# Layer 0's mixer: keys and memory queries projected first, norms spread between k steps, attention in paired halves with the sample as one of its items

## What is computed

```python
z = h @ p['w_in_a'][a]
q, k, v, xq = jnp.split(z, [A_Q, A_Q + A_KV, A_Q + 2 * A_KV], axis=-1)
q = rms_norm(q.reshape(n, t, A_HEADS, HEAD_DIM), p['q_norm_a'][a])
k = rms_norm(k.reshape(n, t, A_KV_HEADS, HEAD_DIM), p['k_norm_a'][a])
v = v.reshape(n, t, A_KV_HEADS, HEAD_DIM)
if is_prompt:
    o = swa_prompt(q, k, v, slopes, p['sinks_a'][a])
else:
    o, nk, nv = swa_sample(q, k, v, win_k_in[a], win_v_in[a], slopes, p['sinks_a'][a])
...
xq = rms_norm(xq.reshape(n, t, X_HEADS, HEAD_DIM), p['xq_norm'][i])
xo = memory_attention(xq, mk, mv)
x = x + jnp.concatenate([o, xo], axis=-1) @ w_out
```

## Time and profile before

| | us |
|---|---|
| median of 3 runs | 2440.69 (2440.61 to 2445.96) |
| span of the profiled execution | 2437.8 |
| PE busy in it | 2364.8 (97%) |
| DVE, ACT, POOL busy | 1152.4, 674.6, 596.1 |

### The profile page before, as it was taken

One profiled execution on the slowest core, in us unless ns is written; L12 is line 12 of the kernel. 1 busy time (PEld: TensorE's weight loads), 2 busy tenths in 40 slices (PEclk: granted clock), 3 DMA queues, 4 the chain that ended last, 5 costly groups with the idle time before them and its releaser, 6 DMA issues.

```text
span 2437.8 us, 37784 instructions
## 1 busy us (share of the span) xinstructions
PE 2364.8 (97%) x14538; PEld 2238.3 (92%) x14538; DVE 1152.4 (47%) x2144; ACT 674.6 (28%) x1247; POOL 596.1 (24%) x413
## 2 busy tenths in 40 slices
PE   5999999999999999999999998899999999999999
PEld 5898755899999999999999997699999999999999
DVE  7213377245454455554455133415555445445554
ACT  6211277242211112222225222514222221112221
POOL 3111033342212122222224121333222221212221
PEclk9998799999999999999999998899999999999999
DMA  5213000111111111111111112011111111111112
GB/s 202 86 44 139 5 1 1 29 44 61 44 43 35 42 47 48 52 52 52 43 35 51 44 44 95 4 43 35 52 53 52 52 43 43 35 42 44 50 52 84
DMA packets 36288, 123.29 MB, mean 51 GB/s; under 512 B 5264, under 2 KB 9968, under 8 KB 34896
## 3 DMA queue, kind: packets, MB, share of 16 engines
q1 hardware_dynamic: 26208, 95.43, 12.7%
q10 hardware_dynamic: 10000, 26.76, 2.9%
HBM read 115.57 MB, written 8.63 MB: 51 GB/s over the span
## 4 chain that ended last, share of the span: by engine, by line
PE 87%; DVE 5%; issue 4%; ACT 2%; POOL 1%; ACTq 0%; DMA 0%; DVEq 0%; POOLq 0%
PE ps L449 26%; PE ps L450 26%; PE ps L451 25%; PE ps L645 2%; DVE h_lo L1258 2%; PE ps L672 2%; PE ps L578 1%; PE ps L659 1%; PE ps L610 1%; ACT s_exp L1014 1%; DVE z L1645 1%; PE ps L722 1%; PE ps L560 1%; ACT p_t L850 0%; DVE s_exp L1424 0%
## 5 line engine op out<-in xcount | busy, mean ns | idle before, releaser
L449 PE MATMUL ps<-h_hi,w_hi 128*128 128x352 f32 x3120 | 1012.7, 325 | 14.9 <-DVE h_lo L1258 5.6
L450 PE MATMUL ps<-h_lo,w_hi 128*128 128x352 f32 x3120 | 1001.5, 321 | 0.0
L451 PE MATMUL ps<-h_hi,w_lo 128*128 128x352 f32 x3120 | 1000.7, 321 | 0.0
L356 POOL TENSOR_TENSOR w_lo<-raw,w_hi 128x1024 fp32r<-128x1024 f32 x138 | 345.1, 2502 | 1497.3 <-ACT w_hi L850 1497.3
L449 PEld LDWEIGHTS ps<-h_hi,w_hi 128*128 128x128 f32 x3120 | 586.3, 188 | 36.5 <-issue 22.3
L450 PEld LDWEIGHTS ps<-h_lo,w_hi 128*128 128x128 f32 x3120 | 587.2, 188 | 0.0
L451 PEld LDWEIGHTS ps<-h_hi,w_lo 128*128 128x128 f32 x3120 | 585.9, 188 | 0.0
L1565 DVE TENSOR_TENSOR x<-x,ps 128x352 f32<-128x352 f32 x528 | 270.7, 519 | 173.9 <-PE ps L451 173.1
L449 PE MATMUL ps<-g_hi,d_hi 128*128 128x352 f32 x1056 | 340.4, 322 | 3.5 <-DVE g_lo L1558 3.5
L450 PE MATMUL ps<-g_lo,d_hi 128*128 128x352 f32 x1056 | 339.9, 322 | 0.0
L451 PE MATMUL ps<-g_hi,d_lo 128*128 128x352 f32 x1056 | 339.7, 322 | 0.0
(11 more groups left out here) (175 smaller groups left out, 1897.0 us busy)
## 6 DMA issues: line engine op xcount, KB each, us to landing
raw<-in_w SPq DMA_DIRECT2D x182, 512.0 KB, 3.6
x<-in_x_t ACTq DMA_DIRECT2D x4, 1056.0 KB, 10.0
out_y<-x ACTq DMA_DIRECT2D x8, 528.0 KB
s_mk<-in_s_mk ACTq DMA_DIRECT2D x2, 2048.0 KB, 9.5
s_mv<-in_s_mv ACTq DMA_DIRECT2D x2, 2048.0 KB, 14.6
mem_x<-in_mem_t ACTq DMA_DIRECT2D x1, 1024.0 KB, 7.0
s_k<-in_s_k ACTq DMA_DIRECT2D x2, 512.0 KB, 4.4
s_v<-in_s_v ACTq DMA_DIRECT2D x1, 1024.0 KB, 17.1
```

The lines of the kernel that those rows point to most:

```text
L356: pool.tensor_tensor(lo, raw[:, slot], hi.bitcast(F32), ALU.subtract).then_inc(prepped, 1)
L449: pe.matmul(out, a, hi_x(k), start=(first and n == 0), stop=False)
L450: pe.matmul(out, a, lo_x(k), start=False, stop=False)
L451: ins = pe.matmul(out, b, hi_x(k), start=False, stop=(last and n == len(ks) - 1))
```

## The change

The in-projection's units come in another order: keys (6, 7), memory queries (8, 9), queries (0 to 5), values (10, 11). All units from the third on write banks 0 to 2, and spreads (`spread_a`) go to banks 3 to 5 between k steps, four tiles in units 5 and 6, six in unit 11; the root is taken twice. Square sums are added inside units. Value transposes (`values_in`) come behind the first item's scores. SyncE issues the cache loads and then the window stores.

The attention has 25 items: per block two sliding-window items of 6 heads (two key heads, one in each half of the partitions) and one memory item of 4 heads, and as item 5 the sample (its four kinds of heads with queries in `q4`, 32 columns each, four samples side by side in the columns). Each item has two halves n = 2k and 2k + 1, which top, exps, scale, normalise, turn and take handle one by one. Scores of an item fill banks 0 to 3. The sink is a column of the scores, so that its maximum, exponential and sum come with the others and the small instructions for it go. Outputs go back into `z` (`evict`), and are cut into high and low parts later in pieces of 128 x 704, eight of them on ScalarE and GpSimd between items, four at the end on ScalarE and VectorE. The first two output chunks of the first output unit run between the last items, and the first six chunks come in the order (0,0), (0,1), (1,0), (1,1), (0,2), (1,2). `p_t` has three places, two of them and `k_tok` over the values in `z`, so that ScalarE waits for the store of those values (`vp_stored`) before it writes `k_tok` or `p_t`. Layer 1 keeps its work; its functions are only separated.

```diff
+NORMED_A = [[6, 7, 8, 9], [0, 1, 2, 3, 4, 5]]
+SPREAD_AT = {(5, 1, 1): 6, (5, 1, 6): 7, (5, 2, 3): 8, (6, 0, 3): 9,
+             (11, 0, 2): 0, (11, 0, 6): 1, (11, 1, 2): 2, (11, 1, 6): 3, (11, 2, 2): 4, (11, 2, 6): 5}
+STAT_AT = {(2, 1): 0, (2, 2): 1, (3, 1): 2, (4, 1): 3, (5, 1): 4, (6, 1): 5, (7, 1): 6, (8, 1): 7, (9, 1): 8,
...
+SMP_AT = 5
...
+def attn_items():
+    out = []
+    for b in range(NB):
+        out += [("swa", b, 0), ("swa", b, 1), ("mem", b, 0)]
+    out.insert(SMP_AT, ("smp", 0, 0))
+    return out
...
-        cursor[0] = r_at + 10 * size([P, T])
-        p_t = put("p_t", [P, 2, 2 * 3 * P])
...
+            for u in range(IN_A):
+                n = S_INA + u
+                sp.wait_ge(prepped, n - 1)
+                sp.dma_start(raw[:, n % 2], d["w"][S_INA + UNITS_A[u]]).then_inc(raw_landed[n % 2], 16)
+            load_units(S_OUTA // 2, S_OUTA // 2 + 1)
+            m = mx[0]
+            sp.wait_ge(proj, 3 * (R_INA + IN_A))
+            for i in range(2):
+                sp.dma_start(s_k[:, i, :, 0:BLOCK], d["s_k"][:, i]).then_inc(m["caches"], 16)
+            sp.dma_start(s_v[:, :, :], d["s_v"]).then_inc(m["caches"], 16)
+            sp.dma_start(s_mk[:, :, :, :], d["s_mk"][0]).then_inc(m["caches"], 16)
+            sp.dma_start(s_mv[:, :, :, :], d["s_mv"][0]).then_inc(m["caches"], 16)
+            sp.wait_ge(freed[(R_INA + IN_A - 1) % 2], 3 * ((R_INA + IN_A - 1) // 2) + 3)
+            sp.dma_start(o["win_v_p"], z[:, 10:12, T - BLOCK:T]).then_inc(vp_stored, 16)
+            sp.wait_ge(m["z_normed"], 30)
...
+            def spread_a(t):
+                m = mx[0]
+                idx = UNITS_A.index(t)
+                grp = 0 if t in NORMED_A[0] else 1
+                pe.wait_ge(m["z_rstd"], grp + 1)
+                if idx >= 1:
+                    pe.wait_ge(m["z_normed"], NCH * idx)
+                for c in range(NCH):
+                    pe.matmul(ps[:, 3 + c, 0:CH], sel_t[32 * c:32 * c + 32, t, :], rstd[32 * c:32 * c + 32, :],
+                              start=True, stop=True).then_inc(m["z_spread"], 1)
...
+                pe.wait_ge(prepped, n + 1)
+                for c in range(NCH):
+                    t0 = c * CH
+                    pe.wait_ge(freed[1 - s], 3 * ((r - 1) // 2) + c + 1)
+                    def between(k):
+                        if (u, c, k) in SPREAD_AT:
+                            spread_a(SPREAD_AT[u, c, k])
+                    products(ps[:, c, 0:CH],
+                             lambda k: w_hi[:, s, k * P:(k + 1) * P], lambda k: w_lo[:, s, k * P:(k + 1) * P],
+                             lambda k: h_hi[:, k, t0:t0 + CH], lambda k: h_lo[:, k, t0:t0 + CH],
+                             range(KD), landed=between).then_inc(proj, 1)
+                    if (u, c) in STAT_AT:
+                        idx = STAT_AT[u, c]
+                        first = idx in (0, len(NORMED_A[0]))
...
+            def values_in():
+                m = mx[0]
+                for q in range(6):
+                    if q >= 2:
+                        pe.wait_ge(m["turned_taken"], q - 1)
+                    bank = 6 + q % 2
+                    for b in ([2 * q, 2 * q + 1] if q < 4 else [8]):
+                        w, t0 = (BLOCK, TS + b * BLOCK) if b < 8 else (TS, 0)
+                        for t in range(2):
+                            at = ((b % 2) * 2 + t) * P
+                            mm = pe.transpose(ps[0:w, bank, at:at + P], z[:, (10 if q < 5 else 6) + t, t0:t0 + w],
+                                              ident[:, :])
...
+            def attention():
+                m = mx[0]
+                def scores(k):
+                    kind, b, i = A[k]
+                    if k >= 1:
+                        pe.wait_ge(m["ready"], 2 * k)
+                        if A[k - 1][0] != "swa":
+                            pe.wait_ge(m["exped"], 2 * k)
...
+                    if kind == "swa":
+                        w = BLOCK if b == 0 else 256
+                        k0 = q0 + BLOCK - w
+                        for j in range(3):
+                            for h in range(2):
+                                rows = slice(64 * h, 64 * h + 64)
+                                mm = pe.matmul(ps[:, 2 * h + j // 2, (j % 2) * 256:(j % 2) * 256 + w],
+                                               z[rows, 3 * i + j, q0:q0 + BLOCK], z[rows, 6 + i, k0:k0 + w],
+                                               start=True, stop=True)
+                                if j == 2:
+                                    mm.then_inc(m["scored"], 1)
...
                 def turn(n):
-                    kind, b, g = items[n]
-                    nh = 3 if kind == "swa" else 2
+                    kind, b, i = A[n // 2]
+                    h = n % 2
                     pe.wait_ge(m["normed"], n + 1)
                     if n >= 1:
                         pe.wait_ge(m["pturned_taken"], n)
                     out = banks(4, 2, 768)
...
+                def values(k):
+                    kind, b, i = A[k]
+                    pe.wait_ge(m["pturned_taken"], 2 * k + 2)
+                    if k == 0:
+                        pe.wait_ge(m["turned_taken"], 6)
+                    if k >= 2:
+                        pe.wait_ge(m["o_done"], k - 1)
...
+                    if kind == "swa":
+                        kcs = [0] if b == 0 else [0, 1]
+                        for kc in kcs:
+                            for h in range(2):
+                                g = 2 * i + h
+                                mm = pe.matmul(ps[64 * h:64 * h + 64, bank, 0:3 * P],
+                                               v_tok[:, b - len(kcs) + 1 + kc, g * HD:(g + 1) * HD],
...
+                                                   pt_sm[:, kc, cs], start=(kc == 0), stop=(kc == 1),
+                                                   skip_group_check=True)
+                    mm.then_inc(m["pv"], 1)
+                pe.wait_ge(freed[0], 3 * ((R_INA + IN_A) // 2))
+                pe.wait_ge(freed[1], 3 * ((R_INA + IN_A) // 2))
+                pe.wait_ge(m["z_normed"], NCH * len(stat_tiles(0)))
+                for k in range(M + 3):
+                    if 2 <= k < M + 2:
+                        turn(2 * k - 4)
+                    if k >= 3:
+                        values(k - 3)
+                    if k < M:
+                        scores(k)
+                    if 2 <= k < M + 2:
+                        turn(2 * k - 3)
+                    if k == 0:
+                        values_in()
+                    if k == M:
+                        pe.wait_ge(m["exped"], 2 * M)
+                        pe.wait_ge(m["o_cut"], 4)
+                        pe.wait_ge(m["o_low_pool"], 4)
+                        pe.wait_ge(prepped, S_OUTA + 1)
+                        out_a_unit(R_OUTA, 0)
+                    if k == M + 1:
+                        pe.wait_ge(m["o_cut"], 8)
+                        pe.wait_ge(m["o_low_pool"], 8)
+                        out_a_unit(R_OUTA, 1)
...
+            def attention():
+                m = mx[0]
+                def exps(n):
+                    kind, b, i = A[n // 2]
+                    h, st = n % 2, stat[:, n % 8]
+                    act.wait_ge(m["ready"], n + 1)
                     if kind == "swa":
...
+                def take(n):
+                    kind, b, i = A[n // 2]
+                    act.wait_ge(m["pturned"], n + 1)
+                    if n == 0:
+                        act.wait_ge(vp_stored, 16)
+                    out = banks(4, 2, 768)
+                    if kind == "smp" and n % 2 == 0:
+                        scopy(pt_sw[:, :, :], out[:, 0:384].rearrange("p (j n) -> p j n", j=3))
+                        ins = scopy(pt_new[:, :, :], out[0:TS, 384:768].rearrange("p (j n) -> p j n", j=3))
+                    elif kind == "smp":
+                        ins = scopy(pt_sm[:, :, :], out[:, 0:256].rearrange("p (k n) -> p k n", k=2))
+                    else:
+                        w = 512 if kind == "mem" else 384 if b == 0 else 768
+                        if n >= 3:
+                            act.wait_ge(m["pv"], (n - 3) // 2 + 1)
+                        ins = scopy(p_t[n % 3][:, 0:w], out[:, 0:w])
+                    ins.then_inc(m["pturned_taken"], 1)
...
+                act.wait_ge(m["sinks_set"], 1)
+                for k in range(M + 2):
+                    for h in range(2):
+                        if k >= 2:
+                            take(2 * k - 4 + h)
+                        if k < M:
+                            exps(2 * k + h)
+                    if k == 0:
+                        values_in()
+                    if k in SPLIT_AT:
+                        high(SPLIT_AT[k])
+                for e in range(8, 12):
+                    high(e)
...
+                def top(n):
+                    kind, b, i = A[n // 2]
+                    h, st = n % 2, stat[:, n % 8]
```

(44 more changed lines are left out.)

990 lines of the change are left out of this document (532 added, 458 removed).

## The result

The changed kernel takes 2477.4 us (median of 4 runs, 2476.0 to 2478.9) where the kernel before took 2440.7 in the same session: 1.0146 times as long, 95% interval 1.0132 to 1.0159. Slower was forecast, by 13 us; it is 36.7. The profiled execution spans 2475.1 us (before: 2437.8), so that the difference to be placed in the traces is 37.3.

What follows compares the result with a forecast made beforehand. TensorE was taken to bound the kernel before. Items to 438.9 plus 16.8 for clock falls put the output projection's first product at 455.7 against 441.5, +14.2; taken as +13 on the median 2440.7: 2454 us, range 2425 to 2475.

Steps and rivals of the forecast that it cites:

- s(k): Attention: time when item k's scores are usable; s(3) 257.5, s(9) 323.1, s(24) 429.1 us without the twelve clock falls.
- Projection: Input projection: in-line norms 8.8, square sum 0.7 and bank wait 1.7 put the last product 11.2 us later, at 227.5.
- The triples: Last projection unit: ten spreads of three matmuls between k steps, each delaying the next product 0.88 us, 8.8 in all.
- The queue of the stores: Attention start: ScalarE waits for the out_win_v_p store behind the cache loads, until 248.5 instead of 236.
- rival 2: Attention start: the store is not held up by the loads, 12 us less, 2442; chance 0.08.
- The items around the sample: Attention from s(3) 257.5 to s(9) 323.1, with 19.9 us of sample values and sample scores at a quarter of 15.8.
- The chain in a paired item: Attention: scores, top, exponentials, copy, turn, values form one loop without overlap; block 21.2 us against 18.9, idle time 3.7.
- rival 1: Attention: the clock holds, since TensorE is active 12.4 of 21.2 us; 16.8 less, 2436; chance 0.18.
- The clock: Attention: each 3.7 us idle time costs a fall, 3.4 us at half clock, losing 1.4; twelve sliding items, 16.8.
- After the last scores: End of attention: TensorE work behind s(24) apart from two output chunks, 6.1, 2.7 and 1.0, in all 9.8 us.
- (4): Attention: the clock stays at half through most of it, 29 us more, 2483; chance 0.11.
- (3): Attention: the loop is not the bound, VectorE's 15.8 us per block counts and no falls; about 2400; chance 0.11.

Runs made afterwards that it cites:

- the kernel with the three edits: Changed kernel with both p_t copies ahead of the exponentials on ScalarE, the out_win_v_p store ahead of the cache loads, and 96 unused bytes: 2414.4 us.
- the pad: Changed kernel with 96 unused bytes per partition put back where the arrays of negated sinks stood: 2465.8 us.
- the run with the two early ones: Changed kernel with unneeded matmuls in twelve sliding items' idle times and the two ahead of the sample, 96 bytes and the store ahead of the loads: 2435.8 us.

## Why the prediction was right in direction and too low in size

The loop in a paired item and the wait for the store came as forecast. What failed were sizes and one missing term. The price of the falls of the clock was too low: none was put on the idle times ahead of the sample (6.5 us low from s(3) to s(9)), and for each one behind it the stretch at half clock was taken as 3.4 us where it is 4.8 on average (5 us low in five blocks). And everything outside the mixer was put at nothing, where the moved tiles cost most of 9.1 us. In the order of the prediction's steps, with s(k) read at the end of the scores' groups:

**Projection: 11.2 forecast, 13.5 measured.** The triples cost what was said: ten intervals of 1.05 between products where 0.16 stood. Unit 2's wait for the fourth eviction is there, 1.70 of idle time at 89. What was missed is the pace: from unit 7 on, where neither memory products nor spreads stand between, a unit takes 12.49 us where it took 12.37. The place of the tiles enters here too: the kernel before takes 12.49 with its 32 bytes added, and the changed kernel 12.40 on average at +128. But it isn't all of it, nor does the place within 128 bytes decide here: with the 96 bytes put back the unit takes 12.54. The cause of that stays open.

**The queue of the stores: right to 0.3.** s(3) was to come 30.0 behind the last product and comes 29.7 behind it (259.5). The chain of what ended last runs there through one piece, the store:

```profile
232.94 16.82 DMA out_win_v_p<-z
249.76 0.02 issue
249.78 0.02 ACTq L1225
249.79 0.04 issue
249.84 0.37 ACT k_tok L1083
```

The rule of the Trainium skill cited for it (DMA: Bandwidth & Descriptors, on queues, rings and completion order), that a DMA's semaphore is written behind every earlier write of the same DMA engine, agrees with the 16.8 behind the loads against 3.2 ahead of them. The price in rival 2 was wrong, though: 12 for 6.0, since what comes next was put at 236 and comes at 241 to 244.

**The items around the sample: 6.5 low.** From s(3) to s(9) 65.6 were forecast without the twelve falls of the clock. Two of these twelve belong to the sliding items 7 and 8 in this stretch (whose s(8) and s(9) hold a part at half clock already), which makes 68.4; measured are 74.9 (334.4). Against the 65.6 these are +2.6 for s(4), +4.2 for s(5), -1.2 for s(6) and s(7), +2.5 for s(8) with the sample's values, +1.3 for s(9). The sample's own terms were near: values 22.2 for 19.9, of which the 64 records of line 852 take 13.80, as in the earlier trace rows. Its scores, the group of line 781, take 6.4 in all with the clock partly down, where the kernel with the three edits needs 5.1; 4.0 had been put there, until their first half is usable. The rest is turns, values and scores of ordinary items at half clock: with all these idle times filled, the two early ones included, the stretch takes 66.0, 0.4 from the forecast without falls. So the falls cost 8.9 us there, and 2.8 had been put. The forecast had put falls of the clock on the twelve sliding items behind the sample only, and full clock on those ahead of it, although they have the same idle times. That is the step that failed here.

**The chain in a paired item: right.** 21.2 forecast, 21.4 measured with the clock held up; idle time 3.7 forecast, 3.76 measured; turning one order breaks the loop. The objection that TensorE is active for more of the block than in the stretches where the clock had fallen (rival 1) was no protection: at 3.76 of idle time it falls, each time.

**The clock: 1.4 per item forecast, 1.9 measured.** Ten sliding items in five blocks cost (25.2 - 21.4) x 5 = 19 us. The window from 332.4 to 458.3 tells why:

```profile
332.40:458.30 125.90, 82.12 (x482) 51.63 (x480) 56.81 (x135) 64.04 (x196) 45.02 (x85) 0.81 0.00 1
```

A mean of 0.81 between 1.00 and 0.50 is 38% of the time at half clock, 48 us, 4.8 for each idle time. The forecast took one stretch of 3.4 from the earlier trace rows for each and lost 1.4 in it, 0.41 of its length; the runs lose 1.9 of 4.8, which is 0.40. So the price of a microsecond at half clock was right, and the length of the stretch was mis-sized: a single row of the kernel before had been taken for all, and its bound of 3.8 was not worked into the middle. The Trainium skill (TensorE: Matmul & The Clock Gate, on the failure mode by cycling through PSUM) describes matmul groups with small idle times between them, whose clock goes to and fro and whose throughput is lost between bursts; this trace agrees, with 1.00 and 0.5 in turn and 19 us lost in 126.

**After the last scores: 1.4 less than forecast.** 9.8 were put there; the first product of the output projection behind the last values (476.5), less the 7.7 of the two chunks that run ahead of them (48 products at the pitch), stands 8.4 behind s(24) at 460.4. With this the 11.7 of the attention are: -0.3 at s(3), +6.5 to s(9), +6.0 in the five blocks (126.0 for 106 and ten falls of 1.4), -1.4 behind, +0.5 for the slower products of the output projection, 11.3 in all.

**The stages behind: 0 forecast, 9.1 measured.** This is the term that was put at nothing. "Everything the change touches in earnest lies in the first" mixer was taken from the instructions. The allocations had been changed as well: 96 bytes less, and all products of 1.9 ms 0.4% slower. About 7.4 of the 9.1 are this pace, 1.6 the fall of the clock in layer 1. In the runs the pad is worth 11.6 and 11.2, of which the pitch accounts for about 8. The rest is probably in single falls of the clock, which come and go from trace to trace: the one in layer 1 is there with 96 bytes put back and missing with 224.

Of the rivals, (4) had the right sign and nearly the total (2483), by a mechanism that is only in part the one seen: the clock is at half for 38% of the blocks, not for most of them. (3) is what the kernel becomes when the order on ScalarE is turned, at 18.0 a block and not 15.8. The range ended 2.4 us below the result. It had been built from the attention's terms alone, and a term for what lies outside of it was not in it.

## What to carry to other kernels

When an engine's program interleaves two roles (here: copies that free banks and exponentials that need new input), write down for each instruction what it waits for and who waits for it, and put first the one that the bounding engine needs; here one such order was worth 44.5 us, more than the 36.7 that the whole change added. An idle time of TensorE is to be priced as its own length plus the slower work behind it, for every place that has it, and unneeded matmuls in the gap are a cheap way to measure that share, sometimes to keep it. After any change to the allocations compare the pace of products in a stage that wasn't touched, and put the tiles back to their old place before judging the rest.

## What the runs showed of the hardware

- The pace of TensorE's products depends on where the tiles lie in a partition: with the tiles behind the small arrays shifted by 0 or +128 bytes a pitch of 159.1 to 159.2 ns, by -96, -64 or +32 bytes 159.8 to 159.9. Over the kernel the pitch makes 8 us, and the medians differ by 10 to 12; at -64 the median is only 7 to 8 above the fast ones. This holds for the feed-forward stages; in the input projection the changed kernel is slower at 0 (12.54 us a unit) than at +128 (12.40). Why was not found, nor which operand.
- The clock also falls while TensorE is busy. In the kernel with the three edits its groups follow each other without idle time from 283.40 on, the last of them the 96 products of the sample's values with 24 and then 8 columns for each 128 x 128 weight; the granted clock goes from 1.00 to half at 288.7, where the 64 of 8 columns begin, and they take 13.80 us. With the gaps ahead of them filled (the last filler from 283.37 to 286.7 in the run with the two early ones) it still falls, at 290.0.
- With idle times of 3.76 that come every 9 to 16 us the stretch at half clock behind them is 3.4 long, or 6.8 at two successive idle times of the same block: 4.8 on average.
